# Layer A by gates, values and heads: values by token with x as the stationary side, gates and values kept in memory and fetched per head

## The chip, the cores and the metric

One Trainium2 chip, of which one core is used. The metric is the device time of one execution in microseconds (us); lower is better. Before the change it is 2071.63 us (median of 3 runs, 2071.57 to 2072.84).

## The reference

Two sequences of 512 tokens (a prompt and a sample, both with the same weights) run through layer A, layer B and a final norm. What the change touches is layer A:

```python
def layer_a(x, mem, ln_g, w_in, mem_ln_g, w_mem, w_out):
    h = rms_norm(x, ln_g)
    z = h @ w_in                       # 1024 -> 3*3*1024 (q, k, v of 3 groups) + 512 + 1536
    qkv, q_mem, gate = z[..., :9216], z[..., 9216:9728], z[..., 9728:]
    y_mix = dilated_mixer(qkv)         # 8 heads of 128; per head 3 groups, each with q, k, v
    y_mem = memory_attention(q_mem, rms_norm(mem, mem_ln_g), w_mem)    # 4 heads
    y = jnp.concatenate([y_mix, y_mem], axis=-1) * jax.nn.silu(gate)
    return x + y @ w_out
```

`dilated_mixer` does, per head and group, a softmax over a window of keys, multiplies by the values and joins the three groups by their log sums.

## The kernel before, in words

The projection `z = h @ w_in` is done by Strassen's scheme in pairs: two blocks of 128 output columns times two halves of 512 tokens, 7 products (numbered 0 to 6) in place of 8. Operand tiles are split in a high and a low part (fp32r), and a product is 3 matmuls (high with high, high with low, low with high) for each of 4 chunks of the contraction: 12 matmuls of 512 columns (`product`, L290; matmuls L315 to L317). The 7 operands on the side of x are made once in the prologue (`h_hi`, `h_lo`) and stay in SBUF. On the side of the weights five quarters of 256 KB are loaded per pair by the SyncE queue (`pair_load`, L248; issue L255), four sums are made on GpSimd (`weight_sum`, L257), and each product's operand is split on ScalarE (high, `op_split_hi`, L277) and VectorE (low, `op_split_lo`, L286) into a ring of 5 slots, in program order four products ahead of TensorE. The weights are the stationary side, x the moving side, so results stand by feature: 128 features on the partitions, 512 tokens along them. ScalarE evicts four of the seven products (L898), VectorE adds three (L907).

`dilated` (L910) runs 8 heads, each of 5 pairs (35 products): q and k of the three groups (pairs 0 to 2), values of groups 0 and 1 (pair 3), values of group 2 and the gate (pair 4). After them come 4 pairs with query and gate of the memory heads: 44 pairs, 308 products, of which the prologue does the first 7.

The attention of a head is laid out by hand between the products, one entry per product index `u`, counted from the head's first product, the same on every engine: scores at 20 to 27 (`scores`, L1044), softmax pieces one product later, joins at 27 and 31 (`join`, L1235, which needs statistics sent through memory by GpSimd, L991 to L1006), turns of the probabilities at 29 to 36 (`turn_probs`, L1064), weighted sums at 35 and 38 (`weighted_values`, L1088), multiplication with the gate at 36 and 39 (`finish`, L1273). Entries from 35 on lie between the products of the next head. Since the weighted sum needs the values by token, six entries (26 to 29, 33 and 35) turn them: four 128x128 transposes into `v_ps` (`turn_values`, L1075, L1084), and a copy on VectorE (`move_values`, L1265, L1270).

Every engine runs its instructions in order. The SyncE queue holds, per head, the loads of the next pair in the order of need and the store of the finished head before it (`store`, L960), which waits for `finish`. GpSimd's order per head (L1014) puts the statistics' transfers between the weight sums. After the heads the block loads what the memory attention needs (L980) and scales it (`memory_row`, L1297).

Of the kernel before, what the change touches and what calls it, by code (L numbers as in the profile page):

```python
# [28 lines left out]
P = 128  # L29
# [3 lines left out]
NS = 2  # L33
# [31 lines left out]
PAIRS_HEAD = 5  # L65
SLOTS_HEAD = OPS * PAIRS_HEAD
OPS_ALL = OPS * (PAIRS_HEAD * DIL_HEADS + MEM_HEADS)
RING = 5
# [48 lines left out]
def build(nc, A):  # L117
    with ExitStack() as top:
# [120 lines left out]
        CHAIN = [z_ps[0][:], z_ps[1][:], z_ps[0][:], z_ps[1][:], s_ps[:, SEQ:2 * SEQ]]  # L239
        SINGLE = [s_ps[:, SEQ:2 * SEQ]] * 4 + [z_ps[0][:]]  # L240
# [15 lines left out]

        def weight_sum(pool, j, n):  # L257

            if n == 1:
                pool.wait_ge(raw_in[0], 16 * j + 16)  # L260
                pool.wait_ge(raw_in[1], 16 * j + 16)
                need(pool, lo_op, OPS * j - 5)
                pool.tensor_tensor(raw["X"], raw["A21"], raw["A22"], ALU.add).then_inc(s_sum, 1)  # L263
            if n == 2:
                pool.wait_ge(raw_in[2], 16 * j + 16)
# [6 lines left out]
            if n == 4:  # L272
                pool.wait_ge(raw_in[3], 16 * j + 16)
# [3 lines left out]
        def op_split_hi(act, j, i, u):  # L277

            if i in (0, 5, 6):
                act.wait_ge(raw_in[{0: 2, 5: 3, 6: 4}[i]], 16 * j + 16)  # L280
            else:
                act.wait_ge(s_sum, 4 * j + {1: 1, 2: 2, 3: 4, 4: 3}[i])
# [7 lines left out]
        def product(pe, h_hi, h_lo, j, p, i, u, arrival=None):  # L290

            out = {0: CHAIN[p], 1: CROSS, 2: CHAIN[p], 3: CROSS, 4: CHAIN[p], 5: SINGLE[p], 6: CHAIN[p]}[i]
            if i == 0 and p in (0, 4):
                need(pe, z_dve, 3 * j)
            if i == 0 and 0 < p < 4:
# [5 lines left out]
            if i == 5 and p == 0:  # L301
                need(pe, z_act, 4 * j)
            if i == 5 and 0 < p < 4:
                need(pe, z_dve, 3 * j)
            if i == 5 and p == 4:
                need(pe, z_act, 4 * j - 4)
# [203 lines left out]
        def prologue(xa, qkv, h_hi, h_lo, early, st):  # L510
# [58 lines left out]
            def _(sp):  # L569
# [15 lines left out]
                pair_load(sp, A["a_win"][0], (0, DIL_W), 0)  # L585
# [4 lines left out]
                pair_load(sp, A["a_win"][0], (3 * DIL_W, 4 * DIL_W), 1)  # L590
# [5 lines left out]
            def _(pool):  # L596
# [6 lines left out]
                for i in range(1, RING):  # L603
# [85 lines left out]
            def _(act):  # L689
# [65 lines left out]
                evict_act(act, qkv, 0, 0, 0, True)  # L755
                high(5)
                evict_act(act, qkv, 0, 0, 1, True)
# [3 lines left out]
                evict_act(act, qkv, 0, 0, 2, True)  # L761
# [4 lines left out]
            def _(dve):  # L766
# [98 lines left out]
                dve.wait_ge(lo_op, RING)  # L865
                op_split_lo(dve, 0, 5, 5)
                evict_dve(dve, qkv, 0, 0, 3, True)
                op_split_lo(dve, 0, 6, 6)
                evict_dve(dve, qkv, 0, 0, 4, True)
                for i in range(2):  # L870
                    op_split_lo(dve, 1, i, 7 + i)
                evict_dve(dve, qkv, 0, 0, 5, True)
# [4 lines left out]
        PLACE = [(0, 1), (2, 3), (4, 5), (6, 7), (6, 2)]  # L877

        def outs(qkv, p, c, s, bank, natural):


            tile = qkv[:, PLACE[p][c], s * SEQ:(s + 1) * SEQ]
            if not natural or (p, c) not in ((0, 0), (0, 1), (3, 0)):
                return [(tile, bank)]
            o, b = tile.rearrange("p (i r) -> p i r", r=RES), bank.rearrange("p (r i) -> p i r", r=RES)
            if (p, c) == (0, 0):
# [4 lines left out]
        def evict_act(act, qkv, j, p, i, natural, func=ACT.Copy):  # L891
# [3 lines left out]
            c, s, bank = {0: (0, 0, CHAIN[p]), 1: (1, 1, CROSS), 2: (0, 1, CHAIN[p]), 6: (1, 0, CHAIN[p])}[i]  # L895
            act.wait_ge(prod, OPS * j + i + 1)
            for o, b in outs(qkv, p, c, s, bank, natural):
# [3 lines left out]
        def evict_dve(dve, qkv, j, p, i, natural):  # L901

            c, s, bank = {3: (0, 1, CROSS), 4: (1, 1, CHAIN[p]), 5: (0, 0, SINGLE[p])}[i]
            dve.wait_ge(prod, OPS * j + i + 1)
            dve.wait_ge(z_act, 4 * j + {3: 3, 4: 2, 5: 1}[i])
            for o, b in outs(qkv, p, c, s, bank, natural):
# [3 lines left out]
        def dilated(qkv, work, h_hi, h_lo, y_stored, ended):  # L910
# [7 lines left out]
            with ExitStack() as st:  # L918
                q0, k0 = qkv[:, 0, :], qkv[:, 1, :]
# [3 lines left out]
                gate = qkv[:, 2, :]  # L923
# [6 lines left out]
                fac_nat = [sb(f"fac_nat{s}", [P, RES], stack=st) for s in range(NS)]  # L930
                stat_mem = [scratch(f"stat_mem{s}", (SEQ, 2)) for s in range(NS)]
# [2114 lines left out]
```

## Time and profile before

| | |
|---|---|
| median of 3 runs | 2071.63 us (2071.57 to 2072.84) |
| profiled execution, its own time | 2072.06 us |
| its span, first to last instruction | 2070.0 us |
| outside the span | 2.06 us |
| mean granted TensorE clock | 0.997 |
| TensorE matmuls, instructions and busy time | 10061, 2026.2 us |
| the block with all heads of layer A | about 75 to 1086 us |

Starts are counted from the first instruction. A matmul's duration is that of its passage through the pipeline: what one costs is the distance from its start to the next start. Idle time is listed with the engine and line that ended it.

### The profile page before, as it was taken

The numbers are of one execution on the slowest core, as the hardware profiler recorded it, in microseconds if no ns is written. First come the engines' busy times: TensorE is split into PE (matmuls) and PEld (weight loads), VectorE is DVE, ScalarE is ACT, GpSimd is POOL, SyncE is SP. The second block draws the span as 40 slices with busy tenths as digits, with TensorE's granted clock in tenths as the row PEclk, the third lists the DMA queues.
The fourth block names the chain that finished last, engine by engine and source line by source line (L and its number), as shares of the span: only waits on it lengthen the run. The fifth ranks groups of instructions, "written<-read, shape, count | busy, mean of one in ns | idle before, by whom it ended". The sixth has DMA issues, their size and how long they took to land. (4 is left out here: it accounts for less than half of the span.)

```text
span 2070.0 us, 28425 instructions
## 1 busy us (share of the span) xinstructions
PE 2026.2 (98%) x10061; PEld 1656.7 (80%) x10061; DVE 1093.8 (53%) x2004; ACT 824.1 (40%) x1489; POOL 405.5 (20%) x343
## 2 busy tenths in 40 slices
PE   7999999999999999999999999999999999999998
PEld 4788888888888888888878788678888888867787
DVE  7655453635445464635445432587878784334312
ACT  6443443534343443534334411545454543223322
POOL 3323232322323232322310011400101010000011
PEclk9999999999999999999999999999999999999999
DMA  7222222222212212222415420411111111512422
GB/s 245 82 57 67 57 51 71 56 68 54 61 51 61 76 47 65 51 72 55 133 51 179 142 67 21 139 31 41 43 39 42 38 44 41 158 51 92 152 61 102
DMA packets 209160, 156.05 MB, mean 75 GB/s; under 512 B 8538, under 2 KB 196420, under 8 KB 208452
## 3 DMA queue, kind: packets, MB, share of 16 engines
q1 hardware_dynamic: 203808, 147.15, 23.6%
q0 software_dynamic: 4480, 6.66, 1.3%
q10 hardware_dynamic: 804, 1.33, 0.2%
q8 instruction: 42, 0.69, 0.1%
q14 instruction: 26, 0.21, 0.0%
HBM read 130.64 MB, written 24.48 MB: 75 GB/s over the span
## 5 line engine op out<-in xcount | busy, mean ns | idle before, releaser
L288 DVE TENSOR_TENSOR w_lo<-w_raw,w_hi 128x512 fp32r<-128x512 f32 x303 | 253.9, 838 | 224.3 <-ACT w_hi L284 223.6
L284 ACT ACTIVATE w_hi<-w_raw 128x512 fp32r<-128x512 f32 x308 | 193.2, 628 | 233.6 <-PE z_ps L317 105.7
L212 PE MATMUL z_ps<-b_parts,w_hi 128*128 128x512 f32 x680 | 274.1, 403 | 3.3 <-ACT g_gate L222 1.8
L214 PE MATMUL z_ps<-b_parts,w_lo 128*128 128x512 f32 x680 | 268.4, 395 | 0.0
L213 PE MATMUL z_ps<-b_parts,w_hi 128*128 128x512 f32 x680 | 268.2, 394 | 0.0
L315 PE MATMUL z_ps<-ah_hi,w_hi 128*128 128x512 f32 x608 | 245.4, 404 | 2.3 <-ACT qkv L898 1.5
L317 PE MATMUL z_ps<-ah_hi,w_lo 128*128 128x512 f32 x608 | 240.4, 395 | 0.0
L316 PE MATMUL z_ps<-ah_lo,w_hi 128*128 128x512 f32 x608 | 239.8, 394 | 0.0
L212 PEld LDWEIGHTS z_ps<-b_parts,w_hi 128*128 128x128 f32 x680 | 128.1, 188 | 36.5 <-issue 7.2
L214 PEld LDWEIGHTS z_ps<-b_parts,w_lo 128*128 128x128 f32 x680 | 128.0, 188 | 30.1
L213 PEld LDWEIGHTS z_ps<-b_parts,w_hi 128*128 128x128 f32 x680 | 128.2, 188 | 28.3 <-issue 0.5
L197 DVE TENSOR_TENSOR w_lo<-w_raw,w_hi 128x1024 fp32r<-128x1024 f32 (+1 forms) x48 | 72.3, 1507 | 135.8 <-ACT w_hi L193 135.8
L315 PE MATMUL t_ps<-ah_hi,w_hi 128*128 128x512 f32 x352 | 142.4, 405 | 0.0
L316 PE MATMUL t_ps<-ah_lo,w_hi 128*128 128x512 f32 x352 | 138.8, 394 | 0.0
L317 PE MATMUL t_ps<-ah_hi,w_lo 128*128 128x512 f32 x352 | 138.7, 394 | 0.0
L315 PEld LDWEIGHTS z_ps<-ah_hi,w_hi 128*128 128x128 f32 x608 | 114.8, 189 | 27.2 <-ACT qkv L898 2.0
L317 PEld LDWEIGHTS z_ps<-ah_hi,w_lo 128*128 128x128 f32 x608 | 114.4, 188 | 26.6
L316 PEld LDWEIGHTS z_ps<-ah_lo,w_hi 128*128 128x128 f32 x608 | 114.6, 188 | 24.3 <-issue 0.2
L898 ACT ACTIVATE qkv<-z_ps 128x512 f32<-128x512 f32 (+2 forms) x132 | 66.0, 519 | 157.5 <-PE z_ps L317 156.1
L263 POOL TENSOR_TENSOR w_raw<-w_raw 128x512 f32<-128x512 f32 x44 | 57.4, 1303 | 325.2 <-DMA w_raw<-in_a_win 289.8
L315 PE MATMUL s_ps<-ah_hi,w_hi 128*128 128x512 f32 x272 | 110.7, 407 | 0.6 <-DVE qkv L907 0.6
L316 PE MATMUL s_ps<-ah_lo,w_hi 128*128 128x512 f32 x272 | 107.3, 395 | 0.0
(455 smaller groups left out, 3863.7 us busy)
## 6 DMA issues: line engine op xcount, KB each, us to landing
w_raw<-in_a_win SPq DMA_DIRECT2D x220, 256.0 KB, 3.1
w_raw<-in_b_win SPq DMA_DIRECT2D x33, 512.0 KB, 4.1
y_scratch<-y SPq DMA_DIRECT2D x16, 512.0 KB, 2.7
w_raw<-in_a_wout SPq DMA_DIRECT2D x8, 768.0 KB, 5.7
w_raw<-in_b_wout SPq DMA_DIRECT2D x8, 768.0 KB, 6.3
xt_scratch<-xb SPq DMA_DIRECT2D x1, 4096.0 KB, 11.8
y_scratch<-g_gate SPq DMA_DIRECT2D x8, 512.0 KB, 3.9
b_wkv<-in_b_wmem SPq DMA_DIRECT2D x8, 512.0 KB, 6.5
```

The source lines that it names most:

```text
L197: dve.tensor_tensor(w_lo[slot][:, 0:nk, :], w_raw[slot][:, 0:nk, :], w_hi[slot][:, 0:nk, :].bitcast(F32), ALU.subtract).then_inc(lo_done, 1)
L212: pe.matmul(z_ps[s][:, 0:width], w_hi[slot][:, k, :], hi[k][:, tok], start=(k == 0), stop=False)
L213: pe.matmul(z_ps[s][:, 0:width], w_hi[slot][:, k, :], lo[k][:, tok], start=False, stop=False)
L214: mm = pe.matmul(z_ps[s][:, 0:width], w_lo[slot][:, k, :], hi[k][:, tok], start=False, stop=(k == nk - 1))
L263: pool.tensor_tensor(raw["X"], raw["A21"], raw["A22"], ALU.add).then_inc(s_sum, 1)
L284: act.activation(op_ring(w_hi, u), op_raw[i], ACT.Copy).then_inc(hi_op, 1)
L288: eng.tensor_tensor(op_ring(w_lo, u), op_raw[i], op_ring(w_hi, u).bitcast(F32), ALU.subtract).then_inc(lo_op, 1)
L315: pe.matmul(out, a_hi[:, k, :], h_hi[:, i, k, :], start=first, stop=False, skip_group_check=True)
L316: pe.matmul(out, a_hi[:, k, :], h_lo[:, i, k, :], start=False, stop=False, skip_group_check=True)
L317: mm = pe.matmul(out, a_lo[:, k, :], h_hi[:, i, k, :], start=False, stop=(k == 3), skip_group_check=True)
L898: part = act.activation(o, b, func)
```

## The change

- The pairs are set anew: 4 pairs of gates first (8 heads, two a pair), then the values, then 8 heads of 3 pairs (q and k of the three groups, 21 products), then the 4 memory pairs as before. Their number stays 44 in work: the values of one group are 7 products of 4 parts, each part 4 token blocks of 128 by 3 matmuls of 512 columns, and three groups make 84 parts of 12 matmuls, as much as 12 pairs.
- Gates go through silu and by a store of 1 MB per pair to memory (`gates_out`).
- In a value product x is the stationary side (128 tokens) and the weights (512 columns: four heads) are the moving side. The result stands by token. The four token blocks accumulate in four PSUM banks, so the bank changes after every third matmul. Weights are loaded in pieces of 128 rows by 512 columns into `work`, 16 sums per group on GpSimd. Evicted values go to memory (`values_out`), four stores of 1 MB per group.
- Per head `head_in` fetches 1.5 MB of values in pieces of 512 bytes (6 transfers) and the gate (0.5 MB), behind the store of the head before on the SyncE queue.
- `turn_values` and `move_values` are gone. The entries of the attention keep their indices (scores at 20, joins at 27 and 31, and so on), now with 21 products to a head, so that most of them lie between the products of the next head. GpSimd's order is kept relative to them.
- The ring has 6 slots (still four products ahead in program order). q0 and k0 have two places, for even and odd heads. The gate has a tile of its own. The head loop runs two heads a turn; heads 0 and 1 and the value part are written out.

```diff
-PAIRS_HEAD = 5
+PAIRS_HEAD = 3
-RING = 5
+RING = 6
...
+                def v_load(sp, g, name):
+                    if g > 0:
+                        sp.wait_ge(lo_op, v_op(g - 1, {"A21": 3, "A11": 4, "A12": 5, "A22": 6}[name], KH - 1) + 1)
...
+                def v_product(pe, g, i, k):
+                    pe.wait_ge(lo_op, u + 1)
+                    for t in range(TPS):
+                        if k == 0:
...
+                            if i in (2, 3, 4):
+                                v_moved_act(pe, g, i - 2, t)
...
+                        out, tok = v_bank(g, i, t), slice(t * P, (t + 1) * P)
+                        pe.matmul(out, h_hi[:, i, k, tok], a_hi, ...)
+                        pe.matmul(out, h_lo[:, i, k, tok], a_hi, ...)
+                        mm = pe.matmul(out, h_hi[:, i, k, tok], a_lo, ...)
...
+                    def head(h, before, last=False):
+                        for p in range(PAIRS_HEAD):
+                            pair_load(sp, w, ..., j + p + 1)
+                        if before is not None:
+                            store(before)
+                        head_in(h)
...
+                    for g in range(NG):
+                        for name, c, s in (("A21", 0, 1), ("A11", 1, 1), ("A12", 0, 0), ("A22", 1, 0)):
+                            if g + 1 < NG:
+                                v_load(sp, g + 1, name)
+                            elif name == "A12":
+                                sp.wait_ge(lo_op, OPS * J_HEAD)
+                                pair_load(sp, w, cols(0, 0), J_HEAD)
+                            values_out(g, c, s)
...
-                    def turn_values(h, m):
...
-                            tr = pe.transpose(v_ps[:, i * P:(i + 1) * P],
-                                              qkv[:, 6 + g % 2, s * SEQ + i * P:s * SEQ + (i + 1) * P], ident[:])
...
-                        pe.wait_ge(v_ready, NG * NS * h + (5 if s == 1 else 6))
+                        pe.wait_ge(v_in, V_IN * h + V_IN)
...
-                    def move_values(h, m):
...
-                            dve.wait_ge(gate_done, h + 1)
+                            dve.wait_ge(gate_in, 16 * h + 16)
...
-                            if gating and 2 * OPS <= u < 2 * OPS + KC:
-                                memory_row(u - 2 * OPS)
+                            if slots > SLOTS_HEAD and u >= slots - KC:
+                                memory_row(u - (slots - KC))
```

## Rows read from the trace of the kernel before

**Rows 1.** The page's first part: TensorE's busy time in the whole span.
```profile
PE 2026.2 (98%) x10061; PEld 1656.7 (80%) x10061; DVE 1093.8 (53%) x2004; ACT 824.1 (40%) x1489; POOL 405.5 (20%) x343
```

**Rows 2.** Windows: us, busy us (count) of PE, PEld, DVE, ACT, POOL; PEclk, DMA, GB/s.
```profile
19.50:23.70 4.20, 4.20 (x8) 1.71 (x7) 4.06 (x11) 2.71 (x6) 0.00 (x0) 0.63 1.14 320
...
75.00:1020.00 945.00, 942.85 (x4606) 783.39 (x4605) 480.63 (x1162) 385.37 (x830) 272.78 (x234) 1.00 0.22 61
...
616.00:734.00 118.00, 118.00 (x579) 98.17 (x578) 60.05 (x146) 48.45 (x105) 33.64 (x29) 1.00 0.21 60
```

**Rows 3.** Waits of TensorE, 58 to 1086 us (total, times, longest): two of four.
```profile
PE z_ps L315 <- ACT qkv L898: 1.5, 1, 1.5
PE t_ps L1072 <- ACT work L1156: 0.8, 1, 0.8
```

**Rows 4.** Timeline of TensorE: first matmuls of three products in a row.
```profile
89.71 0.40 PE L315 MATMUL t_ps<-ah_hi,w_hi 128*128 128x512 f32 x1
...
92.51 0.40 PE L315 MATMUL z_ps<-ah_hi,w_hi 128*128 128x512 f32 x1
...
95.31 0.40 PE L315 MATMUL s_ps<-ah_hi,w_hi 128*128 128x512 f32 x1
```

**Rows 5.** Lines of TensorE, transposes of the values: busy us, mean ns, idle before.
```profile
L1084 PE MATMUL v_ps<-ident,qkv 128*128 128x128 f32 x192 | 28.7, 272 | 0.0
```

**Rows 6.** Timeline of TensorE around two entries with a turn of values.
```profile
506.09 0.60 PE L1084 MATMUL v_ps<-ident,qkv 128*128 128x128 f32 x4
506.45 0.48 PE L315 MATMUL t_ps<-ah_hi,w_hi 128*128 128x512 f32 x1
506.77 0.39 PE L316 MATMUL t_ps<-ah_lo,w_hi 128*128 128x512 f32 x1
...
509.33 0.60 PE L1084 MATMUL v_ps<-ident,qkv 128*128 128x128 f32 x4
509.76 0.60 PE L1072 MATMUL t_ps<-ident,work 128*128 128x128 f32 x4
```

**Rows 7.** Lines of VectorE and ScalarE, 60 to 1086 us (mean ns of one second).
```profile
L288 DVE TENSOR_TENSOR w_lo<-w_raw,w_hi 128x512 fp32r<-128x512 f32 x303 | 253.9, 838 | 224.3 <-ACT w_hi L284 223.6
L1270 DVE COPY work<-v_ps 128x512 f32<-128x512 f32 x48 | 33.0, 688 | 50.6 <-PE v_ps L1084 50.6
L284 ACT ACTIVATE w_hi<-w_raw 128x512 fp32r<-128x512 f32 x303 | 190.1, 628 | 233.2 <-PE z_ps L317 105.7 <-PE s_ps L317 72.6 <-PE t_ps L317 48.5
```

**Rows 8.** DMA issues: transfers, KB each, median us from issue to landing.
```profile
w_raw<-in_a_win SPq DMA_DIRECT2D x220, 256.0 KB, 3.1
mt_scratch<-qkv SPq DMA_DIRECT2D x1, 2048.0 KB, 10.3
work<-mt_scratch SPq DMA_DIRECT2D x1, 2048.0 KB, 9.4
```

**Rows 9.** The line of the weight loads: issue time (ns) and time to landing (us).
```profile
L255 SPq DMA_DIRECT2D w_raw<-in_a_win x220: 367/373/4156, 13.0 to 1053.3; - x110
...
DMA to landing us min/median/max: 2.8/3.1/11.2
```

**Rows 10.** Timeline of VectorE: second join's scaling, in heads 1 and 6; a finish.
```profile
282.57 2.77 DVE L1255 TENSOR_SCALAR work<-work,fac 128x256 f32<-128x256 f32 x4
...
546.61 0.69 DVE L1280 TENSOR_TENSOR y<-o_ps,qkv 128x512 f32<-128x512 f32 x1 [1.14 <-PE o_ps L1101]
...
871.24 2.76 DVE L1255 TENSOR_SCALAR work<-work,fac 128x256 f32<-128x256 f32 x4
```

**Rows 11.** Timeline of TensorE: the turn of probabilities behind it, heads 1 and 6.
```profile
286.55 0.60 PE L1072 MATMUL t_ps<-ident,work 128*128 128x128 f32 x4
...
876.81 0.60 PE L1072 MATMUL t_ps<-ident,work 128*128 128x128 f32 x4
```

**Rows 12.** Timeline of GpSimd: first weight sum behind a finish.
```profile
557.80 1.29 POOL L263 TENSOR_TENSOR w_raw<-w_raw 128x512 f32<-128x512 f32 x1 [12.88 <-DMA w_raw<-in_a_win]
```

**Rows 13.** One line of the prologue's matmuls: duration min/median/max in ns.
```profile
L648 PE MATMUL z_ps<-mg,wk x64: 592/592/1192, 17.8 to 58.6; 128*128 128x512 f32 x64
```

More of the change, by code:

```diff
@@ L960, in store @@
                     def store(h):
+                        there = y_scratch[0][h]
                         sp.wait_ge(y_done, NS * h + NS)
-                        sp.dma_start(y_scratch[0][h], y[:]).then_inc(y_stored, 16)
-                    def head(h, start, before, last=False):
-                        for p in range(start, PAIRS_HEAD):
-                            end = last and p == PAIRS_HEAD - 1
-                            pair_load(sp, w, cols(None, 0) if end else cols(h, p + 1), PAIRS_HEAD * h + p + 1)
-                            if p == 0:
-                                store(before)
@@ new lines, in _ @@
+                    head(0, None)
+                    head(1, 0)
+                    with sp.Fori(2, H8 - 1) as h:
+                        head(h, h - 1)
+                    head(H8 - 1, H8 - 2, True)
+                    for m in range(MEM_HEADS - 1):
+                        pair_load(sp, w, cols(None, m + 1), J_MEM + m + 1)
+                    store(H8 - 1)
+                    for part, there in zip(memory_views(work), (mt_scratch, k_scratch, m_row_scratch)):
+                        sp.dma_start(part, there).then_inc(mem_in, 16)
@@ L1204, in head @@
                                 attention(before, SLOTS_HEAD + u)
-                            if not gating:
+                            if slots == SLOTS_HEAD:
                                 attention(h, u)
-                    head(0, None, OPS, SLOTS_HEAD)
-                    with act.Fori(1, H8) as h:
-                        head(h, h - 1, 0, SLOTS_HEAD)
-                    head(H8, H8 - 1, 0, OPS * MEM_HEADS)
-                    evict(H8, OPS * MEM_HEADS - 1, True)
+                    for u in range(OPS, GATE_SLOTS):
+                        gate_pair(u - 1)
+                        ahead(u + 4)
@@ new lines, in _ @@
+                    for g in range(NG):
+                        for i in range(OPS):
+                            for k in range(KH):
+                                v_moves(g, i, k)
+                                ahead(v_op(g, i, k) + 4)
+                    head(0, 0, None)
+                    head(1, 1, 0)
+                    with act.Fori(2, H8, 2) as h:
+                        head(h, 0, h - 1)
+                        head(h + 1, 1, h)
+                    head(H8, 0, H8 - 1, OPS * MEM_HEADS)
@@ L1301, in memory_row, with evict @@
                                                  op0=ALU.mult, op1=ALU.mult)
[L1303 to L1308 removed]
+                    def evict(h, odd, u):
+                        p, i = u // OPS, u % OPS
+                        if i in (3, 4, 5):
+                            evict_dve(dve, qkv, J_HEAD + PAIRS_HEAD * h + p, (odd + p) % 2, place_of(odd, p), i, p == 0)
```

509 lines of the change are left out of this document (356 added, 153 removed).

## The prediction

> **What bounds the kernel now.** The page comes first: TensorE is busy 98% of the span [rows 1]. A busy share can hide waits inside it, so the next view is the windows. From 75 to 1020 us, which is the heads of layer A, TensorE is busy 942.85 of 945 us at a granted clock of 1.00, while VectorE is busy about half of the time and GpSimd less than a third; in the 118 us of a single head TensorE is never idle, and VectorE has 58 us, ScalarE 70 us to spare [rows 2]. The waits say the same: in more than a thousand us TensorE waits four times, the longest two 1.5 and 0.8 us [rows 3]. So in this stage only what TensorE itself executes has a price, as long as the other engines stay ahead.
>
> What its work costs is read from starts, not from durations. Three products in a row start at 89.71, 92.51 and 95.31, so 12 matmuls take 2.80 us, 0.233 us each, though each is listed with 0.40 [rows 4]. The three go into three different PSUM banks, and the start after a change of bank comes no later than the others. A head of 118 us is thus 35 times 2.80, or 98.0 us of products, and 20.0 us of attention.
>
> **What is removed.** The transposes of the values are 192 instructions, 272 ns each by their duration [rows 5], but they overlap. Where a turn stands alone before a product, the product's second matmul starts at 506.77; without the turn it would start one step of 0.233 after 506.09, so the turn costs 0.45 us. Where other transposes follow, these start 0.43 us after the turn (509.33 to 509.76) [rows 6]. Of a head's six turns the one at entry 28 is alone and five stand before scores, turned probabilities or more of their kind. I take 0.435 us for each; 8 heads with 6 make 48 turns and 20.9 us. All of it lies on the path, since TensorE has no idle time in which they could hide. The 48 copies on VectorE go too, 33.0 us [rows 7], and pay nothing: VectorE is not the bound.
>
> The Trainium skill ("TensorE: Matmul & The Clock Gate", Part 4) gives about 275 ns for a 128x128 transpose inside a kernel, which the duration in the rows agrees with. As a price it would make the saving 192 times 275 ns, an estimate of 52.8 us; the starts in the rows decide against it.
>
> **What is moved at no cost.** The number of matmuls of 512 columns is the same: 44 pairs of 84 before, and 4 gate pairs, 84 value parts of 12, 24 head pairs and 4 memory pairs after. In the value part x is loaded as weights and the weights stream; both are 128x128 against 512 columns as before, each matmul still loads its stationary side, and I take the same 0.233 us. Nothing before shows this order, so it is bounded: no gain, since no step below 0.233 stands in any of these rows and the columns are as many, and at most 0.087 us more on each change of bank, which is what the first matmul after a turn loses against the step (506.45 to 506.77 less 0.233) [rows 6]. I take zero, because a change of bank between plain products is the nearest row and costs nothing [rows 4].
>
> A value part needs one split on each engine, as a product does now (0.63 us ScalarE, 0.84 us VectorE [rows 7]), and the evictions come at the same rate, four and three of seven. 2.8 us cover them.
>
> **The new waits.** Four places decide whether TensorE stays fed.
>
> First, the seam of two value groups (twice). The last quarter of the next group is loaded behind a 1 MB store that waits for the adds of product 5. These come one per part, with the splits between them, so the store goes out some two parts before the end of the group; the quarter is needed by the second product, four parts into the next. That is about 6 parts or 16.8 us of cover. Store and load are 1 MB each; 2 MB took 10.3 us out and 9.4 us in [rows 8], so both together about 10 us, plus four issues of 0.37 [rows 9], a sum of 1.29 [rows 12] and the splits of 1.5: 14.3 us. It fits by 2.5 us. If the transfers took twice as long, 7.5 us would be lost, 15 us at both.
>
> Second, the seam from values to head 0. The first pair's loads wait until every value operand is split, at least four parts before the end: 11.2 us of cover. Five issues (1.9), the median landing of 3.1 [rows 9], sum and splits (2.8) make 7.8 us. With the longest landing of 11.2 it is 15.9, or 4.7 us lost.
>
> Third, the fetch per head. Store, six value transfers and the gate stand on the SyncE queue behind `finish`, ahead of the next loads. `finish` ends at 547.3 [rows 10], eight issues take 3.0 us, and 2.5 MB at 9.4 us for 2 MB take 11.8 us. The weights behind them would land near 561, where their sum now starts at 557.80 [rows 12]. The product that needs it is entry 50, eleven products after `finish`, at 577; sum and splits take 2.8. Some 13 us remain. The values themselves are due at entry 35 of the head, 17 products after the fetch, 47 us. Cost: nothing. Pieces of 512 bytes are also those of the present weight loads.
>
> Fourth, the turned probabilities. `join` hangs on transfers that do not get faster, while TensorE comes to entry 33 three turns, 1.3 us, earlier. The scaling ends at 874.00 in head 6 and the turn starts at 876.81, 2.8 us later; in head 1 it is 285.34 and 286.55, 1.2 us [rows 10, 11]. So 0.1 us is lost in head 1 and nothing in heads like head 6. If the statistics landed 3 us later in every head, 1.5 us each, 12 us in all.
>
> Small edits together: the memory loads at the end come later (3.25 MB, by the same rate 15.3 us after entry 39, which is product 18 of the last 28), and `memory_row` blocks VectorE from product 20 to about 24; the operand it holds up is due at 25. It is just covered. Silu moves out of the heads, six ring slots instead of five, two places for q0 and k0: no engine but TensorE is near its limit, nothing.
>
> **The sum** against the profiled execution: 2072.06 (span 2070.0 and 2.06 around it) less 20.9, plus 1.0 for the first, second and fourth place together, is 2052.2. That execution is 0.43 us above the median of the runs, so I forecast 2052 us, 1.0% less.
>
> **Rivals.**
> Part given back: the seams or the late statistics cost 5 to 15 us; at 10 us the time is 2062. For it speaks the thin margin at the group seam (2.5 us); against it that a longer landing than the median must meet just these places. 0.13.
> All given back (waits of about 20 us, 2071 to 2073, so that the change only moves the work from TensorE's turns to waits): all bounds of the four places would have to be reached together. 0.04.
> Slower: the change of bank. A value part changes the bank after every third matmul, 336 times in all. If each change costs the 0.087 us of the first matmul behind a turn, 29.2 us are added and the time is 2080. The decision lies at 62 ns a change (20.9 over 336); products in a row show none [rows 4]. 0.06. The other form of it is the clock: a matmul of the prologue took 592 ns mostly and 1192 ns at the longest, in a stretch with a mean granted clock of 0.63 [rows 2, 13]. At the lower of the two levels (1.2 against 2.4 GHz) a step takes twice as long, and 9% of the value part's 235 us there would eat the gain. In the heads, where the bank changes with every product, the clock is 1.00 throughout [rows 2]. 0.02.
> The Trainium skill ("TensorE: Matmul & The Clock Gate", "A second HAM failure mode: psum-queue depth-cycling") tells of a kernel that went through PSUM banks in every iteration and idled so often between groups that its clock swung. By that rule the last form holds; the trace here has bank changes without idle time and without a fall.
> More than forecast: a turn is worth its duration, 192 times 272 ns or 52.2 us [rows 5], and the time 2020. Starts speak against it. 0.01.
>
> **The numbers.** Forecast 0.74 (2047 to 2056: the turns between 0.41 and 0.45 us, waits of 0 to 5 us, and some 3 us of present waits that could go). The range of 2046 to 2063 adds most of the part given back. Two tenths of a percent (4.1 us) is what a measurement of this kernel can tell from no change. Faster is 0.74, 0.13 and 0.01, or 0.88; same 0.04; slower 0.08.
>
> **What will show it.** A head's length should fall from 118 us to 21 times 2.80 plus 17.4, or 76.2 us, with TensorE never idle. The value part should last 235 us from first to last matmul with a step of 0.233 at the changes of bank. No transposes into `v_ps` should stand in the heads. In the waits the lines of the value matmuls should hold no more than a few us, and the first product of head 0 none. I am wrong if the step in the value part is above 0.24, if a wait on `w_lo` comes back at every head, or if head 0 or the second and third group start after a pause of several us.

## The result and the profile after

| | before | after |
|---|---|---|
| median, lowest to highest (7 runs each) | 2071.65 us, 2071.45 to 2075.66 | 2057.73 us, 2052.79 to 2065.44 |
| ratio of the medians, 95% interval | | 0.9935, 0.9925 to 0.9945 |
| profiled execution, its span | 2072.06, 2070.0 us | 2058.21, 2056.5 us |
| layer A, from its first product to the first scores of the memory heads | 58.59 to 1086.36: 1027.8 us | 59.06 to 1070.98: 1011.9 us |

The change made the kernel 0.65% faster, 13.9 us by the medians. The forecast was 2052. The scatter is wider: the kernel before stays within 4.2 us here and within 4.1 to 6.2 us on three later occasions, the changed one spreads over 12.6 us here and 6.5 on a second occasion.

The page of the changed kernel, first part, against [rows 1]:
```profile
PE 2011.7 (98%) x9869; PEld 1639.6 (80%) x9869; DVE 1082.8 (53%) x1940; ACT 804.3 (39%) x1463; POOL 418.2 (20%) x343
```
The 192 transposes are gone from TensorE, and the busy share is the same 98%. The windows of the changed kernel (columns as in [rows 2]: length, busy us and count of PE, PEld, DVE, ACT and POOL, then granted clock, DMA share, GB/s) show the heads and the value part together, then the value part, then one head:
```profile
75.00:1000.00 925.00, 920.73 (x4365) 759.12 (x4364) 462.13 (x1074) 359.02 (x792) 280.48 (x228) 1.00 0.33 96
140.37:375.33 234.96, 234.96 (x1009) 189.03 (x1007) 101.06 (x120) 75.58 (x131) 72.28 (x48) 1.00 0.28 94
744.40:820.83 76.43, 76.16 (x384) 63.71 (x383) 43.98 (x117) 31.52 (x78) 23.62 (x21) 1.00 0.32 86
```
The value part takes 235 us without a pause, at the upper clock. From its first product to the next head's a head takes 76.4 to 78.2 us; the one shown takes 76.7 and has 0.27 us of idle time in it, where before the head of [rows 2] had none. TensorE's timeline shows how the value part begins, and how it passes into head 0:
```profile
140.37 0.40 PE L1078 MATMUL o_ps<-w_hi,ah_hi 128*128 128x512 f32 x1
140.60 0.39 PE L1079 MATMUL o_ps<-w_hi,ah_lo 128*128 128x512 f32 x1
140.82 0.40 PE L1080 MATMUL o_ps<-w_lo,ah_hi 128*128 128x512 f32 x1
141.06 0.39 PE L1078 MATMUL v_ps<-w_hi,ah_hi 128*128 128x512 f32 x1
...
375.33 0.39 PE L1080 MATMUL t_ps<-w_lo,ah_hi 128*128 128x512 f32 x1
375.56 0.40 PE L321 MATMUL z_ps<-ah_hi,w_hi 128*128 128x512 f32 x1
```
From the third matmul to the fourth the bank changes, and the step is 0.24 us like the others. 1,008 steps lie between 140.37 and 375.56, which is 0.2333 us each; none of them is over 0.24. Head 0 starts one step behind the last value. The waits of TensorE from 50 to 1080 us (total, times, longest), against [rows 3]:
```profile
PE z_ps L321 <- DVE qkv L913: 3.1, 5, 1.1
PE z_ps L321 <- ACT qkv L904: 1.6, 1, 1.6
PE s_ps L1670 <- PEq L924: 1.5, 1, 1.5
PE t_ps L1280 <- ACT work L1358: 0.8, 2, 0.6
PE z_ps L321 <- PEq L2440: 0.6, 1, 0.6
```
The 1.6, 1.5 and 0.6 us stood in the kernel before as well. Before, one product waited for an add (L913, then L907), and one turn of probabilities for the copy that frees its bank (L1280, then L1072), both in head 1; the product's line in the kernel before is
```profile
PE s_ps L315 <- DVE qkv L907: 0.6, 1, 0.6
```
Now it is five products and two turns.

**Where the time went.** I measure each entry by the distance from the start of its product to the next product's, less the 2.80 us of a product. Entries 32 and 33 each have 0.43 us when the turn costs only its instructions. In the changed kernel entry 32 had 0.82 and 1.18 in heads 1 and 2, and entry 33 had 1.11, 1.73, 1.73, 0.64, 0.94, 0.70, 0.67 and 0.89 in heads 0 to 7. Over 0.43 that is 1.1 and 5.0 us, 6.1 in all. Before, only head 1 had such an excess (its period was 119.73 against 117.85 us, 1.9 us more). A head with no excess takes 117.85 us before and 76.1 in the versions below that have none; 14 products of 2.80 moved out, so the six turns were worth 117.85 - 39.2 - 76.1, or 2.55 us a head, 20.4 us in eight. For layer A: 1027.8 - 20.4 - 1.9 + 6.1 makes 1011.6 us, where 1011.9 was measured. Outside layer A the profiled execution lost 2.3 us: layer A starts 0.5 us later, and what follows it took 1.9 us more. In the profiles of all versions what follows layer A took 980.5 to 985.5 us with the same instructions in it, so this is chance; these 5 us are also a part of the scatter that has nothing to do with the change.

The 6.1 us come about as follows. VectorE's timeline of the changed kernel in head 2 (the second `join`, its scaling, the adds and the splits in their order):
```profile
629.27 0.65 DVE L1486 TENSOR_TENSOR top<-both 128x4 f32<-128x4 f32 x1 [2.82 <-DMA both<-stat_mem]
...
631.30 2.77 DVE L1502 TENSOR_SCALAR work<-work,fac 128x256 f32<-128x256 f32 x4
633.99 0.68 DVE L913 TENSOR_TENSOR qkv<-qkv,t_ps 128x512 f32<-128x512 f32 x1
634.59 1.18 DVE L298 TENSOR_TENSOR w_lo<-w_raw,w_hi 128x512 fp32r<-128x512 f32 x1
635.69 0.68 DVE L913 TENSOR_TENSOR qkv<-qkv,z_ps 128x512 f32<-128x512 f32 x1
```
and TensorE's at the same place:
```profile
631.58 0.63 PE L1280 MATMUL t_ps<-ident,work 128*128 128x128 f32 x4 [0.56 <-ACT work L1358]
...
634.83 0.60 PE L1280 MATMUL t_ps<-ident,work 128*128 128x128 f32 x4
636.50 0.49 PE L321 MATMUL z_ps<-ah_hi,w_hi 128*128 128x512 f32 x1 [1.07 <-DVE qkv L913]
```
Product 34 is the pair's seventh (`i == 6`). It adds into the bank of product 32 and so waits for VectorE's add of that one. The add starts at 635.69. On VectorE it stands behind the second `join`, which waited 2.82 us for a DMA and then scaled for 2.77 us, behind one more add, and behind a split. The turn at entry 33, on which the prediction had its eye, started at 634.83 without a wait on its scaling. It is the product behind the turn that was late. The 1.1 us at entry 32 hang on the same `join` by another engine: the turn there (631.58) waits for a copy on ScalarE, and ScalarE runs that copy behind the weights of the second `join`, for which it stood idle:
```profile
630.16 0.21 ACT L1345 ACTIVATE down<-down 128x8 f32<-128x8 f32 x1 [3.95 <-DVE down L1488]
...
630.86 0.58 ACT L1358 ACTIVATE work<-t_ps 128x512 f32<-128x512 f32 x1
```

The second scaling is also slow in itself. In every head, before and after the change, it takes 2.75 to 2.77 us where the first one of the same size takes 1.17 to 1.19; GpSimd's weight sums run beside it. Those 1.6 us are more than any one excess at entry 33 (1.30 at most), so the late add has two causes, the order on VectorE and the slow scaling.

### The profile page after: what moved, and what is told of

It is laid out like the page before. It is cut to its first block and busy times, and to the rows that moved or that the text cites. A ratio compares the mean times of both kernels' runs of the same rounds, so it can differ in the third digit from the quotient of the medians.

```text
span 2056.5 us, 27177 instructions
## 1 busy us (share of the span) xinstructions
PE 2011.7 (98%) x9869; PEld 1639.6 (80%) x9869; DVE 1082.8 (53%) x1940; ACT 804.3 (39%) x1463; POOL 418.2 (20%) x343
## 5 line engine op out<-in xcount | busy, mean ns | idle before, releaser
L298 DVE TENSOR_TENSOR w_lo<-w_raw,w_hi 128x512 fp32r<-128x512 f32 x219 | 197.7, 904 | 166.1 <-ACT w_hi L294 165.8
L321 PE MATMUL z_ps<-ah_hi,w_hi 128*128 128x512 f32 x512 | 210.0, 410 | 5.3 <-DVE qkv L913 3.1
L323 PE MATMUL z_ps<-ah_hi,w_lo 128*128 128x512 f32 x512 | 202.0, 395 | 0.0
L322 PE MATMUL z_ps<-ah_lo,w_hi 128*128 128x512 f32 x512 | 202.0, 395 | 0.0
L294 ACT ACTIVATE w_hi<-w_raw 128x512 fp32r<-128x512 f32 x224 | 138.3, 625 | 105.5 <-PE z_ps L323 54.0
L904 ACT ACTIVATE qkv<-z_ps 128x512 f32<-128x512 f32 (+1 forms) x104 | 57.6, 562 | 164.2 <-PE z_ps L323 163.6
L321 PE MATMUL t_ps<-ah_hi,w_hi 128*128 128x512 f32 x256 | 103.6, 405 | 0.0
L323 PE MATMUL t_ps<-ah_hi,w_lo 128*128 128x512 f32 x256 | 101.0, 395 | 0.0
L322 PE MATMUL t_ps<-ah_lo,w_hi 128*128 128x512 f32 x256 | 101.0, 394 | 0.0
L2963 ACT ACTIVATE g_E<-g_E 128x2048 f32<-128x2048 f32 x24 | 46.0, 1918 | 101.2 <-DVE g_E L3121 101.2
```

The costliest lines, as they stand in the source:

```text
L294: act.activation(op_ring(w_hi, u), op_raw[i], ACT.Copy).then_inc(hi_op, 1)
L298: eng.tensor_tensor(op_ring(w_lo, u), op_raw[i], op_ring(w_hi, u).bitcast(F32), ALU.subtract).then_inc(lo_op, 1)
L321: pe.matmul(out, a_hi[:, k, :], h_hi[:, i, k, :], start=first, stop=False, skip_group_check=True)
L322: pe.matmul(out, a_hi[:, k, :], h_lo[:, i, k, :], start=False, stop=False, skip_group_check=True)
L323: mm = pe.matmul(out, a_lo[:, k, :], h_hi[:, i, k, :], start=False, stop=(k == 3), skip_group_check=True)
L904: part = act.activation(o, b, func)
```

## The experiments

Theory A: the expected gain of some 20 us is real, and the part that is missing in the profile is the add of product 32 held up in VectorE's order. Theory B, the rival: transposes are worth another amount than the prediction said, or the seams, the fetch or the bank changes eat the rest. Once the runs of the changed kernel turned out to scatter, theory C was added: something at the branch back of the head loop costs TensorE 4 us now and then.

**The changed kernel once more, and the kernel before without the turns.** The first is unaltered. In the second, the weighted sums read a constant; values are still multiplied, but not turned, copied or used, and ScalarE's two waits for the turns go too.
```
-  SC, VT = 20, {26: 0, 27: 1, 28: 2, 29: 3, 33: 4, 35: 5}
+  SC, VT = 20, {}
...
+  pool.memset(work[:, 4096:4096 + NG * NT * HD], 1.0).then_inc(v_ready, 1)
...
-  pe.wait_ge(v_ready, NG * NS * h + (5 if s == 1 else 6))
+  pe.wait_ge(v_ready, 1)
```


> The changed kernel unaltered, as the measure for the others of this call. Its seven runs so far lie between 2052.79 and 2065.44 us with a median of 2057.73. Theory A (the product at entry 34 waits for the adds that stand behind the second join on VectorE, and the join waits for statistics whose landing differs from run to run): again a wide spread, some 2053 to 2065, and in every head a step at entry 33 longer than the 0.43 us that the turn of probabilities costs, 6 us in all. Theory B (the fetch of values and gates disturbs transfers): the same numbers; this run does not tell them apart.

> The kernel before with the six turns of values per head and their copies left out; the weighted sums read a constant in place of the values. Nothing else is moved: still 5 pairs a head, no fetch, no stores of values. Theory A: TensorE saves 48 turns of 0.435 us, 20.9 us, but comes 1.3 us earlier to entry 34 and waits there in every head as in the changed kernel, so 2054 to 2058 us, and the steps at entries 32 and 33 show the excess. Theory B: without fetches no such wait, 2051 us or below.


The unaltered kernel took 2062.06 us (2058.13 to 2064.60), a ratio of 0.9956 (0.9942 to 0.9969). The kernel before without turns took 2049.52 (2047.93 to 2050.59), 0.9894 (0.9880 to 0.9908), or 22.9 us less than the 2072.46 of the kernel before beside it. Its layer A takes 1007.2 us (58.19 to 1065.35), 20.6 less than before, with 2.3 us of excess at entry 33 in place of the 1.9 in head 1. So the 48 turns were worth 21.0 us, 0.44 each: the price by starts holds, and by the transposes' durations it would have been 52. Theory A's 2054 to 2058 missed: it had expected the waits of the changed kernel to appear here in full, and they appear at a third (2.3 of 6.1). B's "2051 us or below" came out, though not its "no such wait". So the earlier arrival of TensorE alone makes a part of the waits; the fetch bears on the rest, as a profile without it shows further down.

The unaltered kernel's profile shows something new, ahead of head 6. TensorE's timeline:
```profile
818.34 0.39 PE L1269 MATMUL s_ps<-qkv 128*128 128x128 f32 x2
821.29 0.49 PE L321 MATMUL z_ps<-ah_hi,w_hi 128*128 128x512 f32 x1 [2.57 <-DVE w_lo L298]
821.63 0.40 PE L322 MATMUL z_ps<-ah_lo,w_hi 128*128 128x512 f32 x1
821.87 0.59 PE L323 MATMUL z_ps<-ah_hi,w_lo 128*128 128x512 f32 x1
822.25 0.63 PE L321 MATMUL z_ps<-ah_hi,w_hi 128*128 128x512 f32 x1
822.68 0.63 PE L322 MATMUL z_ps<-ah_lo,w_hi 128*128 128x512 f32 x1
```
and its windows over the pause and behind it (columns as above):
```profile
818.73:821.29 2.56, 0.00 (x0) 0.00 (x1) 1.69 (x8) 0.55 (x2) 0.00 (x0) 1.00 0.87 269
821.29:825.40 4.11, 4.11 (x11) 3.25 (x12) 0.00 (x0) 1.09 (x4) 1.21 (x1) 0.58 0.53 145
825.40:833.00 7.60, 7.60 (x39) 6.39 (x38) 3.30 (x16) 4.49 (x13) 1.34 (x2) 1.00 0.12 35
```
The product at 821.29 is the first instruction behind the branch back of TensorE's loop, which takes two heads a turn. The profile puts the wait down to a split, but splits run four entries ahead, and that product's operand had been split long before. The branch has a row of its own (duration in ns as min, median and max, then its start). Here it is at this border, and at the border two heads earlier, where nothing stopped:
```profile
L1328 PEldq COMPARE_BRANCH  x1: 6010/6010/6010, 815.0 to 815.0; - x1
...
L1328 PEldq COMPARE_BRANCH  x1: 238/238/238, 662.2 to 662.2; - x1
```
TensorE's sequencer, which reads the program ahead of the engine, met the branch at 815.0, while matmuls for another 3.7 us were still queued. A branch of 0.24 us is hidden behind them. One of 6.01 us is not, and what is left over is the pause. From 815.0 to 821.0 one of the two DMA queues that carry instructions moved
```profile
q8 instruction: 2, 0.03, 3.1%
```
(packets, MB, share), and from 662.2 to 668.2 nothing: the long branch is one for which code is fetched. After 2.57 us without work the granted clock is 0.58 for 4.1 us, and matmuls start 0.43 us apart (822.25 to 822.68) instead of 0.23: the lower of the two levels, 1.2 against 2.4 GHz. Pause and slow matmuls together make this border 4.4 us longer than the others. A pause does not always bring the lower clock: in the next experiment one of 2.70 us was followed by steps of 0.23 at once.

**GpSimd's order.** The second statistics' store goes ahead of the first factors' fetch, so that the second `join` gets its data earlier.
```
   factors_out(h, 1)
+  stats_out(h, 0)
   factors_in(h, 1)
-  stats_out(h, 0)
   stats_in(h, 0)
```


> The changed kernel with one line of GpSimd's order moved: the store of the second half's statistics goes ahead of the load of the first half's factors, which waits for a transfer of its own. Theory A: the statistics land 1.5 to 4 us earlier, the second join no longer sets the start of the product at entry 34, the excess at entries 32 and 33 goes; 2051 us (2049 to 2053) and a spread of 2 us or less. Theory B: no more than 1 us gained, the spread stays.


2064.14 us (2059.77 to 2067.16), 0.9964 (0.9952 to 0.9977): nothing gained. Its waits of TensorE show why:
```profile
PE z_ps L321 <- DVE w_lo L298: 5.2, 2, 2.7
PE t_ps L1280 <- DVE work L1509: 1.8, 3, 0.9
...
PE z_ps L321 <- DVE qkv L913: 0.8, 2, 0.6
```
The wait for the add fell to 0.8 us, and turns at entry 31 now wait for the first scaling by the factors (L1509), whose fetch was pushed back. The wait only moved. Two borders of the loop, 2.5 and 2.7 us, make up the first line.

**Three idle turns put back.** Four transposes of the identity each at entries 28, 29 and 33, which gives TensorE 1.3 us more to do in a head where the values' turns had stood.
```
+  if u in (28, 29, 33):
+      for i in range(TPS):
+          pe.transpose(v_ps[:, i * P:(i + 1) * P], ident[:], ident[:])
```


> The changed kernel with three idle turns (four transposes each, of a constant, into a bank that is free) put back at entries 28, 29 and 33 of each head. TensorE works 24 times 0.435 us or 10.4 us more. Theory A: it then comes to entry 34 as late as before the change and the waits there go, 5 to 6 us, so the kernel is only 4 to 5 us slower than the changed one, about 2062 us. Theory B: 10 us slower, 2068 us.


2064.25 us (2063.04 to 2068.07), 0.9965 (0.9952 to 0.9977). By the medians some 10 us of work more on TensorE cost about 2 us against the unaltered kernel beside it, but both medians hold pauses at borders (this profile has two, worth 4.1 and 4.2 us). The profiles of the heads are the better measure: a head without a pause takes 77.45 us against the 76.15 of one without waits, 10.4 us in eight, and the 6.1 us of waits are gone, which leaves 4.3 us of cost where theory A had said 4 to 5 and B 10. Entry 32 has 0.43 us everywhere, entry 33 the 0.86 of two turns, no more. That is theory A at its place.

**The second half one entry later.** If A holds, the cure is to move work that is not urgent behind the add. The second half's turns go to entries 34 to 37, its sums to 39; its scaling moves one slot behind the `join`, after the add and the split; GpSimd sends the factors after both weight sums.
```
-  TURN = {29: 0, 30: 1, 31: 2, 32: 3, 33: 4, 34: 5, 35: 6, 36: 7}
+  TURN = {29: 0, 30: 1, 31: 2, 32: 3, 34: 4, 35: 5, 36: 6, 37: 7}
...
-  if u in (27, 31):
+  if u in (27, 32):
       join(h, 1 if u == 27 else 0)
-  if u in (30, 34):
-      scale_natural(h, 1 if u == 30 else 0)
-  if u in (36, 39):
+  if u in (27, 33):
+      scale_residues(h, 1 if u == 27 else 0)
+  if u in (30, 35):
+      scale_natural(h, 1 if u == 30 else 0)
+  if u in (36, 40):
...
-  factors_out(h, 0)
   weight_sum(pool, j + 2, 3)
   weight_sum(pool, j + 2, 4)
+  factors_out(h, 0)
```


> The changed kernel with the second half's turns one entry later (turns 34 to 37, weighted sums 39, gating 40), its joining in slot 32 and the scaling of its residue tiles in slot 33 behind VectorE's add of product 32, its natural scaling in slot 35; GpSimd sends the factors after both weight sums. Theory A (the add that product 34 waits for stood behind the joining and scaling): the steps at entries 32 and 33 fall to 0.42 to 0.45 us above 2.80 in every head, the steps after them at most 0.9, which is 6 us less than the kernel unaltered at the same number of stalls at the back edges: 2052 us without one, 2056 with one, 2061 with two. Rival B (the second half's chain of DMAs is late whatever stands where): waits of about 5 us in all turn up at entries 33 to 36 on VectorE's or ScalarE's products, and the time stays at 2058 to 2064 us.

> The second half one entry later, unaltered, as the measure for the two beside it: 2050 to 2058 us, spread 5 to 8 us; a profile may show steps of 2 to 4 us above their like at entry 20 or entry 0 of a head that begins a turn of the loop, and the waits at entries 32 and 33 are under 1 us in all.


2052.69 us (2049.93 to 2057.76), 0.9915 (0.9901 to 0.9929), and on the second occasion 2052.33 (2049.61 to 2055.58), 0.9910 (0.9895 to 0.9925). In both profiles no product of the heads waits but one, in head 2 (0.53 and 0.30 us). The profiled executions took 2049.93 and 2049.61 us. The waits for the add are gone, as theory A said; the runs still scatter over 6 to 8 us. The edit does two things at once, though. It puts the scaling behind the add, and with GpSimd's new order the weight sums no longer run beside the second scaling, which now takes 1.14 us in place of 2.77. Which of the two was needed was not tested.

**The loop written out, alone and with the shift.** The three turns of two heads on TensorE, ScalarE and VectorE become six heads in a row; instructions and order are the same.
```
-  with pe.Fori(2, H8, 2) as h:
+  for h in range(2, H8, 2):
       head(h, 0, h - 1)
       head(h + 1, 1, h)
```


> The changed kernel with the loop over the heads of TensorE, ScalarE and VectorE written out, six heads in a row in place of three turns of two; every instruction and its order is the same, only the branches back are gone, and the fetch of the values stays. Theory C and rival D alike: no step of over 2 us above its like at the borders of the heads, median 2053 to 2059 us, and a smaller spread than the 6 to 12 us of the kernel unaltered, since only the waits at entries 32 and 33 are left (about 6 us in all). Rival E (the fetch holds up weights or other data, and the branch has no part in it): steps 3 to 4 us above their like stay, at 2058 to 2064 us.

> The two edits together: loop written out, second half one entry later. Theories A and C: neither the waits at entries 32 and 33 (6 us) nor the stalls at the back edges (0 to 9 us) are left: 2050 to 2053 us with a spread of 2 us or less, a ratio of 0.990 to the kernel before. If either theory fails, 2056 or more.

> The second half one entry later with the loop written out, unaltered: 2047 to 2050 us again, spread under 4 us, ratio 0.988 to 0.990 to the kernel before; no step over 1 us above its like anywhere among the heads.


Alone: 2053.26 us (2050.14 to 2055.12), 0.9912 (0.9898 to 0.9925); entries 32 and 33 still hold 6.0 us of excess in its profile, and the spread is 5 us where the unaltered kernel's was 12.6 and 6.5 on other occasions. With the shift: 2047.65 (2046.90 to 2050.30), 0.9889 (0.9874 to 0.9904), and again 2048.50 (2047.53 to 2049.51), 0.9888 (0.9873 to 0.9903). This is the fastest version, 23 us below the kernel before beside it and 10 below the first median of the changed kernel; the shift alone, with the loop written out in both, is worth 5.6 us (2053.26 to 2047.65, side by side). Its waits of TensorE from 50 to 1075 us are those that the kernel before had outside its heads, and no others:
```profile
PE z_ps L321 <- ACT qkv L904: 1.6, 1, 1.6
PE s_ps L1674 <- PEq L924: 1.5, 1, 1.5
PE z_ps L321 <- PEq L2444: 0.6, 1, 0.6
```
and the windows (columns as above) show the heads with 0.6 us without work in 925, where the changed kernel had 4.3, and one head without any:
```profile
75.00:1000.00 925.00, 924.37 (x4391) 763.56 (x4390) 457.70 (x1084) 364.43 (x802) 281.22 (x230) 1.00 0.34 96
739.80:815.90 76.10, 76.10 (x388) 63.93 (x386) 42.78 (x117) 31.83 (x78) 23.75 (x21) 1.00 0.35 87
```
VectorE's timeline of this version in head 2 has the add where it belongs, ahead of the scaling:
```profile
627.03 1.25 DVE L1486 TENSOR_TENSOR top<-both 128x4 f32<-128x4 f32 x1
...
629.80 0.69 DVE L913 TENSOR_TENSOR qkv<-qkv,z_ps 128x512 f32<-128x512 f32 x1 [0.26 <-issue]
630.40 0.69 DVE L298 TENSOR_TENSOR w_lo<-w_raw,w_hi 128x512 fp32r<-128x512 f32 x1
631.01 1.14 DVE L1504 TENSOR_SCALAR work<-work,fac 128x256 f32<-128x256 f32 x4
```
With the shift, all eight runs without the loop lie at 2046.9 to 2050.3, and the nine with it at 2049.6 to 2057.8. No profile of a version without the loop has a pause at a border of two heads; three of the nine profiles with it have five between them, worth 4.4, 4.3, 3.0, 4.2 and 4.1 us. At these five borders TensorE's branch lasts 5.7 to 6.1 us, at the other thirteen of the nine profiles 0.21 to 0.24.

**What the branch waits for.** Theory C had it that instructions behind the branch come through the DMA engines and wait behind the fetch of the head's values, which is in flight at that moment. Two tests: every head but the first without that fetch (weighted sums and gating then read head 0's values and gates), once in the changed kernel and once with the shift; and with the shift, all fetches kept but issued behind the next pair's weights, so that they begin some 10 us past the border.
```
-  head_in(h)
+  if isinstance(h, int) and h == 0:
+      head_in(h)
```
```
   pair_load(sp, w, cols(None, 0) if end else cols(h, p + 1), j + p + 1)
+  if p == 0 and before is not None:
+      head_in(before)
 if before is not None:
   store(before)
-head_in(h)
```


> The changed kernel with the fetch of a head's values and gates left out for heads 1 to 7: every head reads those of head 0 (the values of the weighted sums and the gates are then head 0's). Each queue carries 2 MB less a head; the loop, its branch and the order of every engine's other work are unaltered. Theory C (instructions after the branch back come through the DMA engines and wait there behind the fetch): no step over 1 us above its like at entries 20 and 0 of the heads that begin a turn of the loop, about 2052 to 2059 us, with the waits at entries 32 and 33 left or smaller, since the statistics' transfers have less beside them. Rival D (the branch alone costs it, whatever is in flight): a step of 3 to 4 us above its like at one or two of the back edges stays, 2058 to 2064 us.

> The second half one entry later, loop kept, and the fetch of values and gates left out for heads 1 to 7 (the weighted sums and the gating then read head 0's). With the waits at entries 32 and 33 away, what is left to scatter are the stalls at the back edges. Theory C (instructions after the branch back wait behind the fetch): all runs at 2046 to 2050 us, spread under 4 us, like the version with the loop written out. Rival D (the branch costs it whatever is in flight): 2050 to 2058 us with a spread of 5 to 8 us, like the version with the loop and the fetch.

> The second half one entry later, loop kept, all fetches kept, but each issued behind the next load of a weight pair on SyncE's queue, whose last part waits for the split of the fourth entry of the next head: the fetch begins some 4 entries (11 us) past the border between two heads instead of before it. Theory C: all runs at 2046 to 2050 us, spread under 4 us, no step over 1 us above its like at entries 20 and 0. Rival D: 2050 to 2058 us with a spread of 5 to 8 us.


Without the fetch: 2057.92 us (2051.92 to 2058.94), 0.9936 (0.9920 to 0.9951), and with the shift 2054.13 (2048.72 to 2054.99), 0.9914 (0.9900 to 0.9927). Both profiles fell on the fastest run and have no pause at a border; four of the five runs with the shift lie 4.4 to 6.3 us above it. Theory C had said 2046 to 2050 for all of them, so in that form it fails; but no profile shows whether those four had pauses. The profile without the fetch and without the shift still has 4.1 us of excess at entries 32 and 33, where the three with the fetch (unaltered twice, loop written out) have 6.0 to 6.8. By that one profile the fetch makes the waits longer, but is not their only cause. With the fetch moved: 2050.59 (2048.79 to 2051.36), 0.9893 (0.9878 to 0.9909), a spread of 2.6 us. Its profile fell on the slowest of the four runs and has no pause at a border, so the other three can hardly have had one. That speaks for C; four runs are few.

ScalarE shows what the transfers do to a branch. It has the same loop, its branch itself is 0.05 us long, and what counts is when its next instruction comes. In the changed kernel, with the fetch in flight, and in the version with the shift (second occasion), whose branch comes ahead of the fetch:
```profile
L1454 ACTq COMPARE_BRANCH  x1: 45/45/45, 815.0 to 815.0; - x1
L1454 ACTq FUSED_REGOPS  x1: 78/78/78, 820.4 to 820.4; - x1
...
L1454 ACTq COMPARE_BRANCH  x1: 45/45/45, 806.3 to 806.3; - x1
L1454 ACTq FUSED_REGOPS  x1: 78/78/78, 808.8 to 808.8; - x1
```
At all eight borders of the four profiles with the fetch in flight (278 to 286 GB/s moved meanwhile) ScalarE goes on 5.4 to 6.1 us after the branch; at all ten where it is not (3 to 19 GB/s), 2.4 to 2.6 us; in the kernel before, with one head a turn, 0.2 us. The other instruction queue (q14) has a packet between the branch and that next instruction in each of the first two cases and none in the third. That is theory C, on ScalarE and at every turn; it costs little there, since ScalarE has idle time.

TensorE differs in that its branch fetches code in some turns only. In the changed kernel's own profile the seven transfers ahead of head 6 were issued from 813.55 to 819.28, with the border at 821.10, just as in the run with the pause (810.94 to 816.70, border at 818.7); ScalarE stood for 5.4 us, and TensorE's branch took 0.22. So it is shown that the pauses are TensorE's branch, at which code is fetched. What decides whether it must fetch in a given turn stays open. So do the four slow runs without the fetch: if a long branch of TensorE then took the 2.4 to 2.6 us of ScalarE's, an estimate, the 3.7 us of queued matmuls would cover it.

## Why the prediction was right, and where it was off

The direction and the place of the gain were right, and so was the price of what was removed; 2057.7 is inside the range, but outside the 2047 to 2056 of the likeliest case. Of 19.6 us forecast 13.9 came, and 10.4 on the second occasion (2062.06, an us inside the range). What happened was the first rival, part given back: 6 us at the late adds in the profile, 5.7 us above the forecast by the medians. The seams, which that rival names first, gave nothing back; the late second `join`, which it names too, did, by another successor than the prediction had in mind. The loop's pauses were in no part of the prediction, and that the range held them too is luck.

- **Price of a turn.** 0.435 us each and 20.9 us in all were predicted; heads without waits give 20.4, or 0.425 a turn, and the run without turns 21.0. Counting by starts instead of durations was the step that made the forecast.
- **Value part.** 0.233 us a step and 235 us were predicted, 0.2333 and 235.2 measured. The bank changes 336 times without a price, the clock stays at 1.00, and the rival that would have made the kernel slower has nothing for it here. The rule of the Trainium skill ("TensorE: Matmul & The Clock Gate", "A second HAM failure mode: psum-queue depth-cycling") speaks of idling between groups; here there was none, so this case neither confirms nor refutes it.
- **First and second place, the seams.** 2.5 and 3.4 us of margin held; no step at a seam is longer than the others. A loss of 0.9 us had been put down for them, and it was nothing.
- **Third place, the fetch.** No product waits for its weights because of it, as predicted. What the prediction did not see is that its stage now has a loop of two heads a turn, whose branch can stop TensorE, and that the fetch lengthens ScalarE's stop at its branch and, by one profile, the waits at entries 32 and 33; it looked at queues and landing times, not at the instructions. The 3 to 4.4 us a time, once or twice in three of the profiles, are a part of the scatter.
- **Fourth place, the turned probabilities.** This is the step that failed: 0.1 us was predicted and 6.1 came. The prediction took the margins of the turn at entry 33 (1.2 and 2.8 us) and asked when the scaling ends. It did not ask what else stands behind that scaling on VectorE: one more add, a split, and the add that product 34 needs. In the kernel before, that add and product 34 stood like this in head 3:
```profile
522.78 0.68 DVE L907 TENSOR_TENSOR qkv<-qkv,s_ps 128x512 f32<-128x512 f32 x1
...
523.58 0.49 PE L315 MATMUL s_ps<-ah_hi,w_hi 128*128 128x512 f32 x1
```
The product starts 0.13 us behind the add's end, the same as in head 1, where it had waited for the add; over the eight heads it is 0.13 to 0.94 us. So the margin was at most 0.8 us, in every head less than the 1.3 us by which TensorE was to come earlier, and the rows were there to be read. The prediction had reckoned with those 1.3 us, only for the wrong successor.
- **The sum.** 2072.06 - 20.4 + 6.1 - 1.9 (head 1's old excess, which the 6.1 contain anew) + 2.0 (2.3 outside layer A less 0.3 around the span) is 2057.9; the profiled execution took 2058.21.

The Trainium skill ("Runtime: NRT & Kernel Launch", section "Instruction fetch mechanics") says that a taken branch to code outside the small window which an engine holds makes it fetch that code by DMA before it goes on. All five of TensorE's long branches come with packets on an instruction queue, and the pauses go when the branch goes, which agrees; the page gives no duration, and the rows here show branches of 5.7 to 6.1 us and 2.3 to 2.7 us of pause.

## What to carry to other kernels

When work is taken off the engine that bounds the kernel, find on each of the other engines the instruction with the least time to spare before that engine needs it, and read its margin through everything queued ahead of it, not only the last link of the chain that one has in mind. Moving one block of work behind that instruction, and GpSimd's sums out of its way, gave back 5.6 us here. And a change that rolls code into a loop, or doubles a loop's body, has its branch as a part with a price of its own: 0.2 us with one head a turn, up to 6.1 us of branch and 4.4 us of lost time at a border with two, gone when the loop is written out. The branch has its own row in the profile; look there before putting a wait at a border down to the engine that the profile names.

## What was not expected of the hardware

- After a pause of 2.57 us TensorE's granted clock was 0.58 for the next 4.1 us, and a matmul of 512 columns took 0.43 us a step. That cost 1.6 us on top of the pause. After a pause of 2.70 us in another run the steps were 0.23 at once, and behind the waits of up to 1.1 us at entry 33 they were too.
- The first instruction behind ScalarE's branch came 0.2 us later with one head a turn, 2.4 to 2.6 with two, and 5.4 to 6.1 with two and 280 GB/s of transfers in flight.
- Four scalings of 128x256 on VectorE took 1.19 us in the first `join` of head 2 and 2.77 in the second, where GpSimd's weight sums (627.18 to 635.2) run beside them. In the shifted version these sums come earlier, and the longest single scaling there is 0.41 us against 1.98. The line of the scaling in the changed kernel, then in the fastest version (ns, min, median and max):
```profile
L1502 DVE TENSOR_SCALAR work<-work,fac x64: 333/351/1976, 460.5 to 1016.4; 128x256 f32<-128x256 f32 x64
```
```profile
L1504 DVE TENSOR_SCALAR work<-work,fac x64: 333/348/406, 460.4 to 1012.5; 128x256 f32<-128x256 f32 x64
```
The Trainium skill ("SBUF — State Buffer", section "Who interferes with whom") says that a scaling of this kind can take the port pair that VectorE shares with GpSimd, and that whoever comes second waits for the other's whole instruction. A single scaling held up for 1.6 us beyond its 0.35, next to sums of 1.3 us, fits that; the rows do not show which of the two had the ports first (the sum's row starts 0.5 us behind the scaling's, and the scaling ends 0.17 us behind the sum).
